# Moving the compressed units of a sparse attention apart, on one core of Trainium2

## What is computed

```python
o_cmp, p_cmp = compressed_branch(q, kcmp, vcmp, slopes)     # 63 compressed keys
idx = selection_indices(p_cmp, s)                           # top 8 of 16 key blocks, for each group
o_sel = selected_branch(q, kv_heads(ks), kv_heads(vs), idx, slopes)
o_win = window_branch(q, kv_heads(kw), kv_heads(vw), slopes)   # 512 keys back
o = g[..., 0:1] * o_cmp + g[..., 1:2] * o_sel + g[..., 2:3] * o_win
```

## Time and profile before

| | us |
|---|---|
| median of 3 runs | 3379.03 |
| lowest, highest | 3377.59, 3379.45 |
| profiled execution | 3380.16 |
| its span | 3378.0 |
| the stage of the change, in that span | 1061 to 1417 |

### The profile page before, as it was taken

How to read it: one execution, slowest core, us unless ns; L and a number is a source line. 1 busy time by engine, 2 the same in 40 slices (tenths; PEclk the granted TensorE clock), 3 DMA queues, 4 the chain that set the end, 5 groups by cost and what they waited for, 6 DMA issues and landing times.

```text
span 3378.0 us, 38441 instructions
## 1 busy us (share of the span) xinstructions
PE 3189.0 (94%) x16047; PEld 2509.0 (74%) x16047; DVE 1640.0 (49%) x2368; ACT 714.9 (21%) x1194; POOL 75.1 (2%) x147
## 2 busy tenths in 40 slices
PE   4899999996998999799999999989989999999999
PEld 3777865553565888688888888868857888888887
DVE  6425115635113556634444454468985445444445
ACT  3233225521112555521000000021134100000001
POOL 1000000100004000000000000000000000000000
PEclk7989999997888999799999999989989999999999
DMA  7001200011210000112111111101100211111111
GB/s 289 19 18 28 54 25 16 16 63 62 50 39 10 1 1 1 61 46 75 43 47 48 50 50 50 43 13 57 38 15 26 75 50 50 50 50 50 48 39 50
DMA packets 138666, 153.29 MB, mean 45 GB/s; under 512 B 27015, under 2 KB 126251, under 8 KB 137003
## 3 DMA queue, kind: packets, MB, share of 16 engines
q1 hardware_dynamic: 136704, 134.40, 12.7%
q10 hardware_dynamic: 1835, 17.11, 1.3%
HBM read 138.91 MB, written 12.58 MB: 45 GB/s over the span
## 4 chain that ended last, share of the span: by engine, by line
PE 56%; DVE 1%; ACT 1%; issue 0%; DVEq 0%; ACTq 0%
PE ps L1233 43%; PE ps L1210 10%; PE ps L1316 1%; PE ps L1367 0%; PE ps L1353 0%; PE ps L735 0%; DVE sc L2378 0%; PE ps L765 0%; DVE h_low L2382 0%; ACT big L1803 0%; ACT h_high L1821 0%; ACT sc L1824 0%; DVE h_low L2517 0%; DVE big L2514 0%; DVE h_low L2291 0%; PE ps L1190 0%
## 5 line engine op out<-in xcount | busy, mean ns | idle before, releaser
L1233 PE MATMUL ps<-f_high,w_high 128*128 128x512 f32 x1408 | 548.4, 389 | 0.0
L1233 PE MATMUL ps<-f_low,w_high 128*128 128x512 f32 x1408 | 547.8, 389 | 0.0
L1233 PE MATMUL ps<-f_high,w_low 128*128 128x512 f32 x1408 | 547.8, 389 | 0.0
L1210 PE MATMUL ps<-h_high,ring_parts 128*128 128x512 f32 x1024 | 322.5, 397 | 22.4 <-DVE h_low L2382 9.0
L1768 ACT ACTIVATE sc<-sc 128x1024 f32<-128x1024 f32 x44 | 46.7, 1061 | 1237.4 <-DVE sc L2335 1237.2
L1233 PEld LDWEIGHTS ps<-f_high,w_high 128*128 128x128 f32 x1408 | 264.3, 188 | 55.5 <-DVE xt L2523 0.4
L1233 PEld LDWEIGHTS ps<-f_low,w_high 128*128 128x128 f32 x1408 | 264.3, 188 | 55.0
L1233 PEld LDWEIGHTS ps<-f_high,w_low 128*128 128x128 f32 x1408 | 264.3, 188 | 54.7
L2358 DVE TENSOR_TENSOR xt<-ps,xt 128x1024 f32<-128x1024 f32 x176 | 211.6, 1222 | 146.8 <-PE ps L1233 146.8
L1233 PE MATMUL ps<-act_high,w_high 128*128 128x512 f32 x704 | 273.9, 389 | 0.0
L1233 PE MATMUL ps<-act_high,w_low 128*128 128x512 f32 x704 | 273.9, 389 | 0.0
(11 more groups left out here) (367 smaller groups left out, 4615.9 us busy)
## 6 DMA issues: line engine op xcount, KB each, us to landing
ring<-in_ffn_w_gate_dram SPq DMA_DIRECT2D x22, 1024.0 KB, 5.3
ring<-in_ffn_w_up_dram SPq DMA_DIRECT2D x22, 1024.0 KB, 5.3
ring<-in_ffn_w_down_dram SPq DMA_DIRECT2D x22, 1024.0 KB, 4.9
ring<-in_conv_w_pw_dram SPq DMA_DIRECT2D x24, 512.0 KB, 3.8
x_kept<-xt ACTq DMA_DIRECT2D x2, 4096.0 KB, 12.0
xt<-x_kept ACTq DMA_DIRECT2D x2, 4096.0 KB, 12.2
ring<-in_w_mod_dram SPq DMA_DIRECT2D x4, 1536.0 KB, 15.4
ring<-in_w_in_dram SPq DMA_DIRECT2D x10, 512.0 KB, 3.9
```

Source lines behind the costliest of these rows:

```text
L1210: last = mm(bank(banks + half), (hi, lo)[wp_][:, k, :], h_part[rp_][:, k, 512 * half:512 * half + 512], start=k == order[0][0] and p_ == 0 ...
L1233: return mm(o, w, rows, start=start and part_ == 0, stop=stop and part_ == 2)
```

## The change

The list of units is written in another order. From the second block on, C1 goes behind S5 of the block ahead, and C2 behind W1 of its own block: S5, C1, S6, S7, W0, W1, C2, W2 to W7, S0 to S5, and C1 of the next block. The first block keeps C1, C2, W0 and so on. The selections move to W2 (group 0) and W5 (group 1), in all blocks. The counts in the waits on `o_taken` and on the row of the compressed weights are taken from the list. No instruction is added or removed.

```diff
--- before.py
+++ after.py
@@ -460,26 +460,42 @@
         def nsa_table():
 
             units, banks, pieces, turns, rows = [], [0] * 4, 0, 0, 0
-            for o, i in enumerate(NSA_ORDER):
-                for br, kind in enumerate(("cmp", "win", "sel")):
-                    for h in range(0, N_H, 4 if kind == "cmp" else 1):
-                        un = Unit()
-                        un.kind, un.br, un.i, un.o, un.h, un.g, un.n = kind, br, i, o, h, h // 4, len(units)
-                        un.b0 = max(0, i - 4) if kind == "win" else 0
-                        un.blocks = 2 if kind == "cmp" else i + 1 - un.b0
-                        un.w = 256 if kind == "cmp" else P * un.blocks
-                        wide = 2 if i >= 4 else 1
-                        bank_ = (un.n * wide) % 4
-                        un.at = 512 * bank_
-                        un.bank_free = max(banks[bank_:bank_ + wide])
-                        banks[bank_:bank_ + wide] = [un.n + 1] * wide
-                        un.first, un.last = un.h % 4 == 0, kind == "cmp" or un.h % 4 == 3
-                        un.pieces = [(a, min(4, un.blocks - a)) for a in range(0, un.blocks, 4)]
-                        un.piece = pieces
-                        pieces += len(un.pieces)
-                        un.row = rows
-                        rows += kind != "cmp"
-                        units.append(un)
+            order = [(0, 0, 0), (0, 0, 4)]
+            for o in range(TB):
+                for br in (1, 2):
+                    for h in range(N_H):
+                        order.append((o, br, h))
+                        if br == 1 and h == 1 and o > 0:
+                            order.append((o, 0, 4))
+                        if br == 2 and h == 5 and o + 1 < TB:
+                            order.append((o + 1, 0, 0))
+            taken, taken_of, cmp_of = 0, [0, 0], [None, None]
+            for o, br, h in order:
+                i, kind = NSA_ORDER[o], ("cmp", "win", "sel")[br]
+                un = Unit()
+                un.kind, un.br, un.i, un.o, un.h, un.g, un.n = kind, br, i, o, h, h // 4, len(units)
+                un.b0 = max(0, i - 4) if kind == "win" else 0
+                un.blocks = 2 if kind == "cmp" else i + 1 - un.b0
+                un.w = 256 if kind == "cmp" else P * un.blocks
+                wide = 2 if i >= 4 else 1
+                bank_ = (un.n * wide) % 4
+                un.at = 512 * bank_
+                un.bank_free = max(banks[bank_:bank_ + wide])
+                banks[bank_:bank_ + wide] = [un.n + 1] * wide
+                un.first, un.last = un.h % 4 == 0, kind == "cmp" or un.h % 4 == 3
+                un.pieces = [(a, min(4, un.blocks - a)) for a in range(0, un.blocks, 4)]
+                un.piece = pieces
+                pieces += len(un.pieces)
+                un.row = rows
+                rows += kind != "cmp"
+                un.bank_taken = taken_of[un.g]
+                if un.last:
+                    taken += 1
+                    un.taken = taken_of[un.g] = taken
+                if kind == "cmp":
+                    un.ahead = cmp_of[un.g]
+                    cmp_of[un.g] = un
+                units.append(un)
             last_of = [max(un.n for un in units if un.o == o) for o in range(TB)]
             turn_of = []
             for step in range(len(units) + 8):
@@ -1144,8 +1160,8 @@
             def n_values(un):
 
                 o = bank(6 + un.g)
-                if un.first and un.o + un.br:
-                    pe.wait_ge(s.o_taken, 2 * (3 * un.o + un.br - 1) + un.g + 1)
+                if un.first and un.bank_taken:
+                    pe.wait_ge(s.o_taken, un.bank_taken)
                 for m, (a, blocks) in enumerate(un.pieces):
                     pe.wait_ge(s.n_copied, un.turn + m + 1)
                     for b in range(blocks):
@@ -2222,8 +2238,8 @@
                 v.wait_ge(s.n_scored, un.n + 1)
                 r = stat[:, un.n % 16, :]
                 if un.kind == "cmp":
-                    if un.o:
-                        v.wait_ge(s.n_turned, nsa_units[un.n - 18].turn + 1)
+                    if un.ahead is not None:
+                        v.wait_ge(s.n_turned, un.ahead.turn + 1)
                     for m in range(4):
                         ins = v.tensor_tensor_reduce(
                             crow[:, un.g, 64 * m:64 * m + N_CMP], cdist[:, un.i, :],
@@ -2272,15 +2288,15 @@
                         ins = stt(o[:, m, :], src[:, m, 0:N_D], d[:, m:m + 1], o[:, m, :], mul, add)
                     ins.then_inc(s.o_taken, 1)
                     if un.kind == "sel" and un.g == 1:
-                        v.wait_ge(s.o_taken, 6 * un.o + 6)
+                        v.wait_ge(s.o_taken, un.taken)
                         v.nop().then_inc(s.o_made, 1)
 
             for step in range(N_NSA + 5):
                 if step < N_NSA:
                     un = nsa_units[step]
                     n_biases(un)
-                    if un.kind == "win" and un.h in (1, 3):
-                        selection(un.i, un.h // 2)
+                    if un.kind == "win" and un.h in (2, 5):
+                        selection(un.i, un.h // 4)
                 if 0 <= step - 1 < N_NSA and nsa_units[step - 1].kind == "cmp":
                     c_normed(nsa_units[step - 1])
                 if 0 <= step - 4 < N_NSA and nsa_units[step - 4].last:
```

## The result

The changed kernel takes 3404.97 us in the median (3401.70 to 3407.98, 4 runs) against 3378.98 before; the ratio is 1.0076, 95% interval 1.0064 to 1.0089. It is 26 us slower. Forecast were 3398, slower, with a range of 3373 to 3414.

A forecast was written before the change was run, and what follows sets the result against it. TensorE was taken to bound the stage, with 42.4 of 357 us idle. Terms 16.4 + 0.5 + 2.5 = 19.4 us on 3380.16 gave 3399.6, or 3398.4 beside the median; range 3373 to 3414.

The forecast's parts named there:

- One wait of 6.15 us: First block of the kernel before: the prediction named this as the block's one TensorE wait.
- the waits for S7's outputs: Seven borders between blocks: C2's product waits for these outputs, 17.8 us in all, which the change would remove.
- step 6: At a border, counted from C1: selection, C2's normalisation and S7's outputs become one VectorE block of 5.3 us.
- steps 1 and 9: At a border, counted from C1: VectorE blocks of 3.0 and 2.7 us, each making its own TensorE wait.
- the border of blocks 4 and 3: Walked step by step: new waits sum to 6.9 us, 30.5 against 28.4 before, so 2.1 us longer.
- six borders, 7/6 to 2/1: Three walked borders (+2.9, +2.1, +3.2) have a mean of 2.7 us; six borders give 16.4.
- border 1/0: Last border, at half clock: TensorE's work is twice as long and covers most of the waits; +0.5 us.
- first block: Moved selections: 2.5 us gained by W5's scores, then selection 1 stretched beside GpSimd, a 5.2 us wait; +2.5 us net.
- I take the same losses to the clock as before: At each walked border: no further loss to the clock was added, the idle time being in more waits but larger.
- The first (the spread works, 3366): Rival, 15%: other units between C1, C2 and S7 give TensorE work during VectorE's extras; faster, 3366 us.
- The second (no difference, 3374 to 3386): Rival, 17%: border waits hide in half-clock stretches or sum to what goes; first block's gain and loss cancel.
- The third (the clock falls a block earlier): Rival, 10%: spread waits put block 1 at half clock, some 14 us longer; 3412, up to 3430 with block 2.

The follow-up runs named there:

- e4: e3 with the selection of group 0 at W0 instead of W2 in all blocks but the first; 3377.67 us.
- f1: The changed kernel with ScalarE's two jobs in a step exchanged, copies before exponentials; 3364.05 us.
- f4: The changed kernel without GpSimd's pooling sums, scalings and subtraction, so the pooling branch is not computed; 3387.09 us in its only run.
- e3: The changed kernel with the selections of the first block alone put back to W1 and W3; 3398.79 us.
- g2: The new order with the selections at W1 and W3 in all blocks and ScalarE's copies first; 3354.86 us.
- f2: The kernel before the change with ScalarE's two jobs in a step exchanged, copies first; 3356.40 us.
- f3: e4 with ScalarE's two jobs in a step exchanged, copies first; 3338.26 us.

## Why the prediction was right, and where not

**The bound and the aim** were read rightly: the stage's length moved by 24.0 us and the profiled span by 22.4, its stage having started 1.7 us earlier; the waits for S7's outputs (17.8 us) went, and came back under other names. "One wait of 6.15 us" in the first block was too short a list: two waits for the normalisation stand ahead of it (3.3 and 2.1 us), but both kernels have them.

**The mechanism** is shown in each of its two halves. That step 6 piles up: e4 moves one selection out of it and regains 21 us. That copies behind the exponential make the further waits: f1 exchanges the two and the waits of that name go from 30 us to nothing. That the extras in steps 1 and 9 wait on their own is seen at the border of blocks 4 and 3, below.

**The border of blocks 4 and 3.** Walked were waits of 1.35, 2.65, 1.5 and 1.4. Measured were 0.76 and 0.47, 2.15, none, and 1.26. The first came in two pieces, the larger at the scores bank that I had put inside it. The third is not there, because TensorE behind the second runs at half clock and reaches C2's product later. The border grew by 3.75 us (32.80 for 29.05, from the scores that stand two units ahead of the old C1 to S0's): 1.5 of it idle, 2.3 busy time at the lower clock (0.90 for 0.94). I had 2.1.

**The terms of the sum**, from the starts of TensorE's scores:

| term | forecast | measured |
|---|---|---|
| six borders, 7/6 to 2/1 | +16.4 | +0.7, +2.5, +0.5, +3.8, +3.1, +3.4 = +13.9 |
| border 1/0 | +0.5 | +5.3 |
| first block | +2.5 | +4.4 |
| between borders and end | 0 | +0.4 |
| stage | +19.4 | +24.0 |

That the sum came within 5 us is in part luck: the three wide borders (7/6 to 5/4) together cost 4.6 us less than the 8.2 put down for them, the three narrow ones (4/3 to 2/1) 2.0 more than theirs, the last one 4.8 more and the first block 1.9 more. The first wide border was walked at +2.9 and measured +0.7; TensorE is idle 3.9 us there, against 3.8 before. My reading is that work behind a wait runs at half clock and leaves less to wait for, as at the third wait above; no run isolates it.

The largest error is the last border. The step that failed is "TensorE's work is twice as long there and covers most". Its idle time went from 3.4 to 7.9 us. The 0.50 that I went by is of a window behind this border; over the border itself the granted clock is 0.64 before and 0.65 after. The half clock came only in the middle of it, and where it was in force TensorE still waited:

```profile
1402.00:1409.00 7.00, 4.79 (x31) 4.41 (x31) 4.07 (x18) 2.83 (x9) 0.00 (x0) 0.84 0.00 0
1409.00:1416.00 7.00, 4.83 (x23) 4.38 (x23) 4.26 (x24) 1.68 (x7) 0.00 (x0) 0.50 0.01 4
```

```profile
1415.40 0.69 PE L1156 MATMUL ps<-ident,ht 128*128 128x128 f32 x2 [1.77 <-DVE ht L2267]
1418.68 1.19 PE L1170 MATMUL ps<-big,sc 128*128 128x128 f32 x4 [1.61 <-ACT sc L1734]
1424.56 0.66 PE L1174 MATMUL ps<-big,sc 128*128 128x65 f32 x2 [1.18 <-ACT sc L1734]
```

A window or selected unit of block 0 is so short (two score matmuls, one transpose, two products) that doubling it covers little of an extra of 2 to 5 us.

**The first block** had both waits as described: 3.6 us before C1's outputs and 5.7 before 1100, selection 1 lasted from 1088.1 to 1095.5, 7.4 us where I had 6.8. TensorE was 2.9 us ahead at W7's scores (31.4 for 34.3 us after the stage's start) and 4.4 behind at S0's. Of the 4.4 us, 3.3 are idle time (14.9 for 11.6) and 1.1 busy time. Mis-sized was mostly what follows the wait: transposes of 0.74 us took 1.30 at half clock. I had put such a loss in the bound and not in the sum. With f4, GpSimd's long instructions are shown to be the cause: without them, those of VectorE take 0.19 and 0.17 us. That the cause is an interface that the two engines share is not shown by any run here.

**The clock.** "I take the same losses to the clock as before" was the second wrong step: of 24.0 us, 8.1 are TensorE's busy time. The idle part alone, 15.9, is under the 19.4 forecast, so the walk was if anything too dear and the clock made up for it. From e3 to e4 the same shows the other way: 12.9 of 19.7 us are busy time.

**The rivals.** The first (the spread works, 3366) did not come true in this kernel, and the price of its condition is now known: with the selection at W0 the same order gives 3378, and with the copies first 3338. The rule from the Trainium skill (Perfetto Trace Analysis, Optimization Strategy), that interleaving regimes may help, is not borne out by the change as it was made. The order alone with the copies first gave 1.5 us (g2 against f2); the order with other places for the selections gave 18 (f3 against f2), of which the order's share is open. The second (no difference, 3374 to 3386) is out by the time: the fastest run took 3401.70. The third (the clock falls a block earlier) did not happen in the profiled execution: S0 to S5 of block 1 take 7.0 us in the change and 7.2 before. It can happen: in the profiles of e3 and e4 they take 9.2.

## What to carry to other kernels

When units are moved in a pipelined list, write down for each step what the helping engine does beside its regular job, and look at neighbouring steps together: two short extras that used to share a wait can each make one, and one that stands behind another stretches it. Then look at the order of jobs inside a step on the engine in between. A copy that is ready should not queue behind an exponential whose input is late; that exchange, without a new buffer, gave 23 us in the kernel before and 41 in the changed one. Together with the new order and the selections at W0 and W4 it makes the fastest version here: 3333.75 us, 45 under the kernel before.

## What the runs showed of the hardware

- Small waits can cost twice. At the border of blocks 4 and 3 the wait of 2.97 us before, and the one of 2.15 after, was followed by eight products that took 1.81 us for 1.06. In e3 against e4 the busy time differs by more than the waits themselves (12.9 and 6.8 us). The border of blocks 7 and 6, with 3.9 us idle, was granted 0.91 in the change; in f3, with 1.0 us idle, 1.00.
- VectorE instructions of 0.17 to 0.19 us lasted 1.0 to 2.4 us beside GpSimd's long ones in the first block, `TENSOR_SCALAR` with one input from SBUF as well as `TENSOR_TENSOR` with two; `MAX8` and `TENSOR_REDUCE` beside them kept their 0.18 and 0.20.
- The stage starts at 1056 to 1058 or at 1060 to 1062 us in the profiles, in kernels that have the same instructions up to there, and runs of one kernel fall into groups 5 us apart (f1: 3361.4, 3361.6, 3366.5, 3366.5). Where this comes from was not looked into.
